# VectorE instead of GpSimd splits the first layer's gate, up and first down weights; two weight copies move ahead of a normalisation

## The chip, the cores and the metric

The kernel runs on one core of a Trainium2 chip. The metric is the device time of one execution in microseconds. A core has a matrix engine (TensorE), three engines for elementwise work (VectorE, ScalarE, GpSimd) and a queue engine (SyncE); each works through its own list of instructions in order, and they wait for each other on semaphores. A weight matrix passes from memory through three of them before TensorE can use it.

## The reference

A trunk of two layers on 512 tokens of width 1024. Each layer has a mixer and a feed-forward part, both with a modulation computed from a vector `c`:

```python
mod = silu(c) @ ada_w[layer] + ada_b[layer]        # six vectors of 1024
x = layer_norm(ALPHA * x + (1 + g_m) * mixer(x * (1 + sc_m) + sh_m))
hf = x * (1 + sc_f) + sh_f
yf = (silu(hf @ w1) * (hf @ w3)) @ w2              # w1, w3: 1024 x 2816, w2: 2816 x 1024
x = layer_norm(ALPHA * x + (1 + g_f) * yf)
```

The change touches the feed-forward part: the gate and up products (`w1`, `w3`) and the down product (`w2`).

## The kernel before

Every operand of TensorE is split into two parts, a high part of lower precision and the low rest; a product is three matmuls (low times high, high times high, high times low). Weights come in slots of 128 x 1024 through rings of four buffers each:

1. SyncE loads a slot into `raw` when the split of the slot four before it is done (`w_lo_ready`).
2. ScalarE copies it to `w_hi` when it has landed and TensorE is done with the slot four before it (`slot_done`); this is the copy (L903).
3. GpSimd computes `w_lo = raw - w_hi`; this is the split (L832).
4. TensorE waits for both.

**The gate and up steps** (`ffn`). Eleven steps per layer, four slots each: slots 0 and 1 hold gate weights, 2 and 3 up weights, for 256 hidden columns. TensorE makes 96 matmuls a step. ScalarE applies silu to the gate (L1261), VectorE multiplies with the up result (L2677, the step's products) and forms four sums of the blocks of the result (L2682 to L2687), which a Strassen-like scheme of seven products for the down matrix needs. For the same scheme VectorE combines four blocks of down weights per step (L2660 to L2666, `combos`); ScalarE issues the load and the store of these.

In the first layer VectorE also computes the second layer's modulation in this loop: four modulation products per step from step 1 on (L2717, L2720), each over a 512 KB slab in one of two buffers `ada_raw`. SyncE's queue in the loop is fixed (L764 to L771): for u = 0 to 3, wait for the split of slot u one step before, load slot u, wait on `ada_step`, load a slab. The slab with number 4j+36+u is loaded when the product of slab 4j+34+u is done, so the weight load of slot 3 of step j comes behind that step's first modulation product, the next step's slots 0, 1 and 2 behind the second, third and fourth.

**The down stage** (`down`). 42 slots per layer (N_DOWN), numbered m from the stage's first slot, of 12 matmuls, or 6 at the short ones. In the first layer GpSimd splits m = 0 to 3 (below LO_FROM) and 30 to 41 (from LO_TO), VectorE the rest; slots 38 and 39 (HELD) go to a place of their own. ScalarE's list there has the copies (`hi`), the high parts of the operands (`b2_hi`, two operations per hidden chunk), and between slots 33 and 36 two normalisations of finished row blocks (`normalize(0)`, `normalize(1)`), each of which waits for VectorE's statistics (L2539).

Of the kernel before, what the change touches and what calls it, by code (L numbers as in the profile page):

```python
# [17 lines left out]
ALU = mybir.AluOpType  # L18
ACT = mybir.ActivationFunctionType
F32 = mybir.dt.float32  # L20
# [19 lines left out]
RING = 4  # L40
# [58 lines left out]
HALF_K = FC // 2  # L99
# [9 lines left out]

DOWN = down_slots()  # L110
N_DOWN = len(DOWN)
LO_FROM, LO_TO = 4, 30
HELD = 38


# [37 lines left out]
SLOTS, N_USED = slot_table()  # L153
# [77 lines left out]
def build_program(nc, wstream, astream, xT, vecs, const, const0, wa_up, dsel, rel, ln_rows, out):  # L231
# [3 lines left out]
    def sem(name):  # L235
        if name not in sems:
            sems[name] = ctx.enter_context(nc.semaphore(name))
        return sems[name]
# [588 lines left out]
    @block.gpsimd  # L827
    def _(pool):
        def split(s, slot):

            pool.wait_ge(sem("w_hi_ready"), s + 1)
            nc.gpsimd.tensor_tensor(w_lo[:, slot, :], raw[:, slot % RAW, :], w_hi[:, slot, :].bitcast(F32),  # L832
                                    ALU.subtract).then_inc(sem("w_lo_ready"), 1)

        assert RAW == RING

        def split_range(a, b):
            if b - a < 2 * RING:
                for s in range(a, b):
                    split(s, s % RING)  # L840
                return
            up, down = -(-a // RING) * RING, b // RING * RING
            for s in range(a, up):
                split(s, s % RING)
            with pool.Fori(up // RING, down // RING) as i:
                for u in range(RING):
                    split(RING * i + u, u)
            for s in range(down, b):
                split(s, s % RING)

        pool.wait_ge(sem("w_lo_ready"), len(FIRST))
        at_ = len(FIRST)
        for x in sorted(list(extra) + [DOWN0, DOWN1]):
            split_range(at_, x)
            at_ = x + 1
            if x in extra:
                pool.wait_ge(sem("w_hi_ready"), x + 1)
                nc.gpsimd.tensor_tensor(extra[x][1], raw[:, x % RAW, :], extra[x][0].bitcast(F32), ALU.subtract
                                        ).then_inc(sem("w_lo_ready"), 1)
                continue  # L860
            for s in range(x, x + LO_FROM):
                split(s, s % RING)
            pool.wait_ge(sem("w_lo_ready"), x + LO_TO)
            for m in range(LO_TO, N_DOWN):
                pool.wait_ge(sem("w_hi_ready"), x + m + 1)
                down_lo(nc.gpsimd, x, m).then_inc(sem("w_lo_ready"), 1)
            at_ = x + N_DOWN
        pool.wait_ge(sem("in_rows"), 16)
        for tb in range(1, TB - 1):
            pool.wait_ge(sem("xh_ready"), TB * 3 + tb + 1)  # L870
            nc.gpsimd.tensor_tensor(x_rows(tb), x_rows(tb), by_chunk(rows_gb[:, 0, :]), ALU.mult).then_inc(sem("scaled"), 1)
            pool.wait_ge(sem("scaled"), tb)
            nc.gpsimd.tensor_tensor(x_rows(tb), x_rows(tb), by_chunk(rows_gb[:, 1, :]), ALU.add).then_inc(sem("out_ready"), 1)
# [3 lines left out]
    def _(act):  # L877
# [41 lines left out]
        def warm_sqrt():  # L919

            nc.scalar.activation(warm[:], eps_col, ACT.Sqrt)
# [261 lines left out]
        def down(layer):  # L1183

            d = SLOTS[f"down{layer}"][0]
            normalize = normalizer(2 * layer + 1)

            def hi(m):
                to_hi(d + m, (d + m) % RING)

            def a_hi(k):

                act.wait_ge(sem("s_step"), 4 * (HALF_K * layer + k + 1))
                if k < 2:
                    act.wait_ge(sem("combo_stored"), 16 * HALF_K * (layer + 1))
                else:
                    act.wait_ge(sem("slot_done"), d + 3 * (k // 2 - 1))
                nc.scalar.activation(a_hl[k % 4][:, 0, :], hid_cols(k, 0, 3), ACT.Copy).then_inc(sem("x_hi_ready"), 1)

            def b1_hi(k):  # L1200

                act.wait_ge(sem("x_ready"), N_SPLIT * layer + SPLIT["a", k])
                nc.scalar.activation(hid_parts(k, 0, 2), hid_cols(k, 3, 2), ACT.Copy).then_inc(sem("x_hi_ready"), 1)

            def b2_hi(k):

                if k == 0:
                    act.wait_ge(sem("slot_done"), d + 15)
                nc.scalar.activation(hid_parts(k, 2), hid_cols(k, 5), ACT.Copy)
                nc.scalar.activation(a22_hi(k), hid_cols(k, 6), ACT.Copy  # L1210
                                     ).then_inc(sem("x_hi_ready"), 1)

            a_hi(0)
            a_hi(1)
            for g in range(6):
                hi(3 * g + 3)
                for k in (2 * g + 2, 2 * g + 3):
                    if k < HALF_K:
                        a_hi(k)
                for k in (2 * g, 2 * g + 1):  # L1220
                    if k < HALF_K:
                        b1_hi(k)
                if g == 5:
                    act.wait_ge(sem("slot_done"), d + 16)
                    for r in range(2):
                        i = nc.scalar.activation(p1_kept(r), by_half(ps[:, 2 * r, :]), ACT.Copy)
                    i.then_inc(sem("p1_copied"), 1)
                hi(3 * g + 4)
                hi(3 * g + 5)
            for k in range(HALF_K):  # L1230
                hi(21 + k)
                b2_hi(k)
            hi(32)
            hi(33)
            warm_sqrt()
            normalize(0)
            hi(34)
            hi(35)
            normalize(1)
            for m in range(36, N_DOWN):  # L1240
                hi(m)
            done[0] = d + N_DOWN
            if layer == 1:
                normalize(2)
                normalize(3)
# [871 lines left out]
    def _(dve):  # L2117
# [528 lines left out]
        def ffn(layer, rest):  # L2646
# [18 lines left out]
                dve.wait_ge(sem("combo_step"), before + 3)  # L2665
                V.tensor_tensor(b21, b21, b11, ALU.subtract).then_inc(sem("combo_step"), 1)  # L2666

            def step(j, between=None):

                combine_weights(j)  # L2670
                if between:
                    between()
                for b in range(2):
                    dve.wait_ge(*((sem("bank_full"), 2 * j + f0) if b == 0 else (sem("slot_done"), 4 * j + (s0 + 4))))
                    dve.wait_ge(sem("silu_ready"), 2 * j + (FC * layer + 1 + b))
                    split = lambda ap: ap.rearrange("q (o a x) -> q o a x", o=1, x=256)
                    V.tensor_tensor(block(j, (slice(0, 5, 4), slice(3, 7, 3))[b]), split(tmp[:, b, :]), split(ps[:, up + b, :]), ALU.mult  # L2677
                                    ).then_inc(sem("prod_ready"), 1)
                a11, s1, s2, a12, a21, s3, a22 = (block(j, a) for a in range(7))
                before = 4 * j + 4 * HALF_K * layer  # L2680
                dve.wait_ge(sem("prod_ready"), 2 * j + (FC * layer + 2))
                V.tensor_tensor(s1, a21, a22, ALU.add).then_inc(sem("s_step"), 1)  # L2682
                V.tensor_tensor(s3, a11, a21, ALU.subtract).then_inc(sem("s_step"), 1)
                dve.wait_ge(sem("s_step"), before + 2)
                V.tensor_tensor(s2, s1, a11, ALU.subtract).then_inc(sem("s_step"), 1)  # L2685
                dve.wait_ge(sem("s_step"), before + 3)
                V.tensor_tensor(a21, a12, s2, ALU.subtract).then_inc(sem("s_step"), 1)  # L2687
# [21 lines left out]

            def two_steps(it, between=None):  # L2710

                for u in range(2):
                    for k in range(4 * u, 4 * u + 4):
                        dve.wait_ge(sem(f"ada_landed{k % 2}"), 64 * it + 16 * (12 + k // 2 + 1))
                        if k:
                            dve.wait_ge(sem("ada_step"), 8 * it + (40 + k))
# [2 lines left out]
                        else:  # L2719
                            V.tensor_scalar(ada_acc[:], ada_raw[:, 0, :], c_act[:, 0:1], None, ALU.mult  # L2720
                                            ).then_inc(sem("ada_step"), 1)
                    if u:
                        dve.wait_ge(sem("ada_step"), 8 * it + 48)
                        fold_rows()
                    step(2 * it + (u + 1), between if u else None)

            with dve.Fori(0, FC // 4 - 1) as it:
                two_steps(it)
# [12 lines left out]
        def down(layer):  # L2741
# [3 lines left out]
            def lo(m):  # L2745

                dve.wait_ge(sem("w_hi_ready"), d + m + 1)
                if m == LO_FROM:
                    dve.wait_ge(sem("w_lo_ready"), d + m)
                down_lo(V, d, m).then_inc(sem("w_lo_ready"), 1)  # L2750

# [11 lines left out]
                                ALU.subtract).then_inc(sem("x_ready"), 1)  # L2763

            for g in range(6):
                if 3 * g + 3 >= LO_FROM:
                    lo(3 * g + 3)
                for k in (2 * g + 2, 2 * g + 3):
                    if k < HALF_K:
# [14 lines left out]
                        ins = V.tensor_tensor(u2_kept(r), p1_kept(r), by_half(ps[:, 5 + 2 * r, :]), ALU.add)  # L2784
                    ins.then_inc(sem("kept_added"), 1)
                lo(3 * g + 5)
            for k in range(HALF_K):
                if 21 + k < LO_TO:
                    lo(21 + k)
                b2_lo(k)  # L2790

        ffn(0, norm(0, "out0"))
        gate_col(1)
# [225 lines left out]
```

## Time and profile before

| | before |
|---|---|
| median of 3 runs | 1326.59 us (1326.4 to 1327.08) |
| profiled execution | 1326.98 us, span 1325.2 us |
| TensorE matmul busy | 1254.8 us (95%) |
| VectorE busy | 901.2 us (68%) |
| ScalarE busy | 528.5 us (40%) |
| GpSimd busy | 476.5 us (36%), 157 splits of 2.54 us on average at L832 |
| chain that ended last | TensorE 60%, issue 17%, GpSimd 9%, VectorE 8%, DMA 3% |

The profiled execution is 0.39 us above the median. Busy shares are averages over stages of different make-up, and a busy matrix engine is not one at its peak, since matmuls overlap. An idle engine costs time only where another one waits for it, so the profile is read stage by stage. The gate and up steps of the first layer lie at about 300 to 545 us of the span, its down stage at 556 to 670, that of the second layer at about 1201 to 1318.

### The profile page before, as it was taken

The page shows a single profiled execution, that of the slowest core. Times are in us where ns is not written, and L with a number is a line of the kernel's source. Part 1 is how long each engine was busy: PE and PEld are TensorE (multiplying, and loading weights), DVE is VectorE, ACT ScalarE, POOL GpSimd, SP SyncE. Part 2 cuts the span into 40 slices and gives each one's busy share as a digit, 9 for nine tenths or more (in the row PEclk, how much of TensorE's full clock was granted, in tenths as well). Part 3 has the DMA queues.
Part 4 walks back from the last instruction along what each step waited for, and adds up shares of the span by engine and source line. Part 5 has one row for each costly group of instructions (what it writes and reads, how often), then busy time and mean ns, then how long its engine had stood idle before and what let it go on. Part 6 is the DMA issues. An engine that isn't in the chain of part 4 may idle for free.

```text
span 1325.2 us, 17193 instructions
## 1 busy us (share of the span) xinstructions
PE 1254.8 (95%) x6298; PEld 1038.9 (78%) x6298; DVE 901.2 (68%) x1244; ACT 528.5 (40%) x767; POOL 476.5 (36%) x195
## 2 busy tenths in 40 slices
PE   7999999998999999599899999999999999999996
PEld 6878887787787778488687777888888888888874
DVE  5489768868778777667766633358697636447785
ACT  3443364542212122366552455527342222225653
POOL 0243332423444444300645332222245444442046
PEclk9999999999999999799999999999999999999998
DMA  9981654534687777557446542212156665645843
GB/s 333 188 175 65 222 160 128 190 112 165 248 286 275 264 281 270 189 152 236 129 164 230 159 124 92 64 63 75 39 176 251 226 233 203 214 173 162 245 151 116
DMA packets 129362, 239.51 MB, mean 181 GB/s; under 512 B 18523, under 2 KB 83307, under 8 KB 126356
## 3 DMA queue, kind: packets, MB, share of 16 engines
q1 hardware_dynamic: 110792, 188.07, 45.5%
q10 hardware_dynamic: 18508, 50.62, 10.5%
q8 instruction: 38, 0.62, 0.2%
q14 instruction: 24, 0.20, 0.0%
HBM read 212.11 MB, written 27.59 MB: 181 GB/s over the span
## 4 chain that ended last, share of the span: by engine, by line
PE 60%; issue 17%; POOL 9%; DVE 8%; DMA 3%; ACT 1%; POOLq 0%; SPq 0%; DVEq 0%; ACTq 0%
PE ps L1391 10%; PE ps L1393 10%; PE ps L1392 10%; POOL w_lo L832 8%; PE ps L1441 4%; PE ps L1442 4%; PE ps L1443 4%; DMA ada_raw<-astream 2%; PE ps L1590 2%; PE ps L1591 2%; PE ps L1592 2%; PE ps L1556 1%; PE ps L1558 1%; PE ps L1557 1%; PE ps L1943 1%
## 5 line engine op out<-in xcount | busy, mean ns | idle before, releaser
L832 POOL TENSOR_TENSOR w_lo<-raw,w_hi 128x1024 fp32r<-128x1024 f32 x157 | 397.7, 2542 | 655.1 <-ACT w_hi L903 654.9
L903 ACT ACTIVATE w_hi<-raw 128x1024 fp32r<-128x1024 f32 (+1 forms) x235 | 238.9, 1031 | 498.2 <-DMA raw<-wstream 181.6
L1391 PE MATMUL ps<-h_lo,w_hi 128*128 128x512 f32 (+2 forms) x1064 | 399.5, 375 | 15.9 <-POOL w_lo L832 13.9
L1393 PE MATMUL ps<-h_hi,w_lo 128*128 128x512 f32 (+2 forms) x1064 | 394.6, 371 | 0.0
L1392 PE MATMUL ps<-h_hi,w_hi 128*128 128x512 f32 (+2 forms) x1064 | 394.6, 371 | 0.0
L1391 PEld LDWEIGHTS ps<-h_lo,w_hi 128*128 128x128 f32 (+1 forms) x1064 | 200.9, 189 | 57.3 <-issue 20.0
L1393 PEld LDWEIGHTS ps<-h_hi,w_lo 128*128 128x128 f32 (+1 forms) x1064 | 200.7, 189 | 34.8
L1392 PEld LDWEIGHTS ps<-h_hi,w_hi 128*128 128x128 f32 (+1 forms) x1064 | 200.9, 189 | 33.2
L650 POOL TENSOR_TENSOR w_lo<-raw,w_hi 128x1024 fp32r<-128x1024 f32 (+1 forms) x20 | 44.6, 2250 | 160.0 <-ACT w_hi L903 159.8
L2717 DVE SCALAR_TENSOR_TENSOR ada_acc<-ada_raw,c_act,ada_acc 128x1024 f32<-128x1024 f32 x35 | 58.8, 1679 | 45.1 <-DMA ada_raw<-astream 44.6
L2677 DVE TENSOR_TENSOR hid<-tmp,ps 128x512 f32<-128x512 f32 (+1 forms) x44 | 29.1, 683 | 86.2 <-PE ps L1393 86.2
L650 DVE TENSOR_TENSOR w_lo<-raw,w_hi 128x1024 fp32r<-128x1024 f32 (+1 forms) x52 | 57.6, 1121 | 30.8 <-ACT w_hi L903 30.4
L1441 PE MATMUL ps<-w_hi,hid_r 128*128 128x512 f32 x160 | 63.9, 400 | 8.2 <-issue 7.6
L2148 DVE SCALAR_TENSOR_TENSOR ada_acc<-ada_raw,c_act,ada_acc 128x1024 f32<-128x1024 f32 x35 | 60.8, 1737 | 12.0 <-DMA ada_raw<-astream 10.1
L1441 PE MATMUL ps<-w_hi,a_hl 128*128 128x512 f32 x132 | 52.5, 398 | 14.4 <-DVE mod L2154 14.4
L1442 PE MATMUL ps<-w_hi,hid_r 128*128 128x512 f32 x160 | 63.6, 398 | 0.0
L1443 PE MATMUL ps<-w_lo,hid_r 128*128 128x512 f32 x160 | 63.6, 398 | 0.0
L1442 PE MATMUL ps<-w_hi,a_hl 128*128 128x512 f32 x132 | 52.2, 395 | 0.0
L1443 PE MATMUL ps<-w_lo,a_hl 128*128 128x512 f32 x132 | 52.1, 394 | 0.0
L2685 DVE TENSOR_TENSOR hid<-hid 128x256 f32<-128x256 f32 (+1 forms) x22 | 48.1, 2186 | 1.6
L1441 PEld LDWEIGHTS ps<-w_hi,hid_r 128*128 128x128 f32 x160 | 30.8, 193 | 16.7 <-issue 9.3
L1590 PE MATMUL ps<-w_hi,h_lo 128*128 128x512 f32 (+1 forms) x112 | 41.8, 373 | 0.7 <-DVE kc L2807 0.7
(318 smaller groups left out, 2033.5 us busy)
## 6 DMA issues: line engine op xcount, KB each, us to landing
raw<-wstream SPq DMA_DIRECT2D x161, 512.0 KB, 4.5
ada_raw<-astream SPq DMA_DIRECT2D x80, 512.0 KB, 4.5
combos<-wstream ACTq DMA_DIRECT2D x22, 1024.0 KB, 5.5
combo_scratch<-combos ACTq DMA_DIRECT2D x22, 1024.0 KB, 3.9
raw<-combo_scratch SPq DMA_DIRECT2D x88, 256.0 KB, 3.3
raw<-wstream SPq DMA_DIRECT2D x66, 256.0 KB, 3.8
ada_first<-astream SPq DMA_DIRECT2D x16, 256.0 KB, 6.7
ada_first<-astream SPq DMA_DIRECT2D x8, 512.0 KB, 10.5
```

The lines of the kernel that those rows point to most:

```text
L650: return engine.tensor_tensor(w_lo[:, s % RING, 0:n], raw[:, s % RAW, 0:n], w_hi[:, s % RING, 0:n].bitcast(F32), ALU.subtract)
L832: nc.gpsimd.tensor_tensor(w_lo[:, slot, :], raw[:, slot % RAW, :], w_hi[:, slot, :].bitcast(F32), ALU.subtract).then_inc(sem("w_lo_ready"), 1)
L903: nc.scalar.activation(w_hi[:, slot, 0:n], raw[:, slot, 0:n], ACT.Copy).then_inc(sem("w_hi_ready"), 1)
L1391: pe.matmul(o, w_h, x_l, start=start, stop=False)
L1392: pe.matmul(o, w_h, x_h, start=False, stop=False)
L1393: return pe.matmul(o, w_l, x_h, start=False, stop=stop)
L1441: pe.matmul(o, x_lo, w_h, start=begin, stop=False, skip_group_check=True)
L1442: pe.matmul(o, x_hi, w_h, start=False, stop=False, skip_group_check=True)
L1443: return pe.matmul(o, x_hi, w_l, start=False, stop=end, skip_group_check=True)
L1590: pe.matmul(o, h_lo[:, k, tokens], w_hi[:, s % RING, w], start=start, stop=False)
L2148: V.scalar_tensor_tensor(ada_acc[:], src, c_act[:, k:k + 1], ada_acc[:], ALU.mult, ALU.add).then_inc(sem("ada_step"), 1)
L2717: V.scalar_tensor_tensor(ada_acc[:], ada_raw[:, k % 2, :], c_act[:, k:k + 1], ada_acc[:], ALU.mult, ALU.add).then_inc(sem("ada_step"), 1)
```

## The change

In the first layer VectorE does the splits of the gate and up slots from the second step on, and of the down slots m = 0 to 3: `step_lo(j, u)` splits slot u of step j, where u = 4 to 6 are the next step's slots 0 to 2. The four modulation products of a step are parted into two pairs (`ada(u, part)`), and the splits stand behind them and behind the combining. GpSimd keeps the first step's four slots. In both layers LO_TO goes from 30 to 32, so that VectorE splits m = 30 and 31 too. ScalarE's copies in the down stage are brought forward: `b2_hi` comes in pairs, slot 34 stands ahead of the first normalisation and slot 36 ahead of the second.

```diff
-LO_FROM, LO_TO = 4, 30
+LO_FROM, LO_TO = 4, 32
@@ GpSimd
-            split_range(at_, x)
+            split_range(at_, x if x != DOWN0 else SLOTS["ffn0"][0] + RING)
...
-            for s in range(x, x + LO_FROM):
-                split(s, s % RING)
+            if x == DOWN1:
+                for s in range(x, x + LO_FROM):
+                    split(s, s % RING)
@@ ScalarE, down
-            for k in range(HALF_K):
-                hi(21 + k)
-                b2_hi(k)
-            hi(32)
-            hi(33)
+            for n in range(6):
+                hi(21 + n)
+                for k in (2 * n, 2 * n + 1):
+                    if k < HALF_K:
+                        b2_hi(k)
+            for m in range(27, 34):
+                hi(m)
             warm_sqrt()
+            hi(34)
             normalize(0)
-            hi(34)
             hi(35)
+            hi(36)
             normalize(1)
-            for m in range(36, N_DOWN):
+            for m in range(37, N_DOWN):
@@ VectorE, ffn
-            def step(j, between=None):
-
+            def step_lo(j, u):
+
+                if layer == 0:
+                    slot = (s0 + u) % RING
+                    dve.wait_ge(sem("w_hi_ready"), 4 * j + (s0 + u + 1))
+                    V.tensor_tensor(w_lo[:, slot, :], raw[:, slot, :], w_hi[:, slot, :].bitcast(F32), ALU.subtract
+                                    ).then_inc(sem("w_lo_ready"), 1)
+
+            def step(j, between=None, beside=None):
+
+                if beside:
+                    beside(0)
+                if not isinstance(j, int) or j:
+                    step_lo(j, 3)
+                elif layer == 0:
+                    dve.wait_ge(sem("w_lo_ready"), s0 + RING)
+                step_lo(j, 4)
                 combine_weights(j)
+                if beside:
+                    beside(1)
+                step_lo(j, 5)
+                step_lo(j, 6)
...
-                for u in range(2):
-                    for k in range(4 * u, 4 * u + 4):
+                def ada(u, part):
+
+                    for k in range(4 * u + 2 * part, 4 * u + 2 * part + 2):
...
+                for u in range(2):
+                    step(2 * it + (u + 1), between if u else None, lambda part: ada(u, part))
@@ VectorE, down
-                if 3 * g + 3 >= LO_FROM:
+                if 3 * g + 3 >= LO_FROM or layer == 0:
                     lo(3 * g + 3)
...
-            for k in range(HALF_K):
-                if 21 + k < LO_TO:
-                    lo(21 + k)
-                b2_lo(k)
+            for n in range(6):
+                lo(21 + n)
+                for k in (2 * n, 2 * n + 1):
+                    if k < HALF_K:
+                        b2_lo(k)
+            for m in range(27, LO_TO):
+                lo(m)
```

VectorE's list in the loop over the first layer's steps, one step up to its products, in the kernel before (`ada_raw`: the slab; `combos`: the down weights that are combined; `hid`: the step's result; register instructions left out):

```order
L2720 TENSOR_SCALAR ada_acc<-ada_raw,c_act 128x1024 [waits ada_landed0]
...
L2717 SCALAR_TENSOR_TENSOR ada_acc<-ada_raw,c_act,ada_acc 128x1024 [waits ada_step]
...
L2660 TENSOR_TENSOR combos<-combos 128x2x256 [waits combo_landed]
...
L2666 TENSOR_TENSOR combos<-combos 128x2x256 [waits combo_step]
...
L2677 TENSOR_TENSOR hid<-tmp,ps 128x2x256
```

The same step after the change:

```order
L2744 TENSOR_SCALAR ada_acc<-ada_raw,c_act 128x1024 [waits ada_landed0]
...
L2741 SCALAR_TENSOR_TENSOR ada_acc<-ada_raw,c_act,ada_acc 128x1024 [waits ada_step]
...
L2677 TENSOR_TENSOR w_lo<-raw,w_hi 128x1024 [waits w_hi_ready]
...
L2677 TENSOR_TENSOR w_lo<-raw,w_hi 128x1024 [waits w_hi_ready]
...
L2664 TENSOR_TENSOR combos<-combos 128x2x256 [waits combo_landed]
...
L2670 TENSOR_TENSOR combos<-combos 128x2x256 [waits combo_step]
...
L2741 SCALAR_TENSOR_TENSOR ada_acc<-ada_raw,c_act,ada_acc 128x1024 [waits ada_step]
...
L2677 TENSOR_TENSOR w_lo<-raw,w_hi 128x1024 [waits w_hi_ready]
...
L2677 TENSOR_TENSOR w_lo<-raw,w_hi 128x1024 [waits w_hi_ready]
...
L2700 TENSOR_TENSOR hid<-tmp,ps 128x2x256
```

All four modulation products stood together at the head of the step and no instruction of the step waited for `w_hi_ready`; now two pairs of splits stand in the list, one behind the first pair of modulation products and one behind the second, and all four wait for ScalarE's copies.

ScalarE's list in the first layer's down stage, from the copy of slot 33 to that of slot 37, before (L921: the table load and a first use of the square root; L1133 to L1149: a normalisation; the last of them is on `xa`):

```order
L903 ACTIVATE w_hi<-raw 128x1024 [waits slot_done,raw_landed2]
L921 ACT_TABLE_LOAD
...
L1133 ACTIVATE cols<-mv,vec_eps 128x1 [waits mv_ready]
...
L1149 ACTIVATE xa<-xa,nmr,rstd 128x8x128 [waits nmr_ready]
L903 ACTIVATE w_hi<-raw 128x1024 [waits slot_done,raw_landed3]
L903 ACTIVATE w_hi<-raw 128x512 [waits slot_done,raw_landed0]
L1133 ACTIVATE cols<-mv,vec_eps 128x1 [waits mv_ready]
...
L903 ACTIVATE w_hi<-raw 128x1024 [waits slot_done,raw_landed1]
```

and after:

```order
L904 ACTIVATE w_hi<-raw 128x1024 [waits slot_done,raw_landed2]
L922 ACT_TABLE_LOAD
...
L904 ACTIVATE w_hi<-raw 128x1024 [waits slot_done,raw_landed3]
L1134 ACTIVATE cols<-mv,vec_eps 128x1 [waits mv_ready]
...
L1150 ACTIVATE xa<-xa,nmr,rstd 128x8x128 [waits nmr_ready]
L904 ACTIVATE w_hi<-raw 128x512 [waits slot_done,raw_landed0]
L904 ACTIVATE w_hi<-raw 128x1024 [waits slot_done,raw_landed1]
L1134 ACTIVATE cols<-mv,vec_eps 128x1 [waits mv_ready]
```

The copy of slot 34 (`raw_landed3`) stands ahead of the first normalisation instead of behind it, that of slot 36 (`raw_landed1`) ahead of the second.

## Rows read from the trace of the kernel before

**Rows 1.** Busy time by stretch: length, then each engine's busy us, clock, DMA share, GB/s.
```profile
318.93:526.12 207.19, 196.03 (x873) 158.56 (x872) 160.16 (x135) 45.92 (x54) 91.95 (x36) 0.98 0.76 271
```
**Rows 2.** Timeline of VectorE: start, length, line, operation, count, idle before and its releaser.
```profile
318.93 0.75 DVE L2720 TENSOR_SCALAR ada_acc<-ada_raw,c_act 128x1024 f32<-128x1024 f32 x1
...
404.40 1.28 DVE L2677 TENSOR_TENSOR hid<-tmp,ps 128x512 f32 x2
...
409.29 2.51 DVE L2687 TENSOR_TENSOR hid<-hid  x1
...
411.79 0.74 DVE L2720 TENSOR_SCALAR ada_acc<-ada_raw,c_act 128x1024 f32<-128x1024 f32 x1
412.56 1.29 DVE L2717 SCALAR_TENSOR_TENSOR ada_acc<-ada_raw,c_act,ada_acc 128x1024 f32<-128x1024 f32 x1
415.94 1.28 DVE L2717 SCALAR_TENSOR_TENSOR ada_acc<-ada_raw,c_act,ada_acc 128x1024 f32<-128x1024 f32 x1 [2.08 <-DMA ada_raw<-astream]
...
427.07 0.69 DVE L2666 TENSOR_TENSOR combos<-combos 128x512 f32<-128x512 f32 x1
...
526.12 2.66 DVE L2717 SCALAR_TENSOR_TENSOR ada_acc<-ada_raw,c_act,ada_acc 128x1024 f32<-128x1024 f32 x2
```
**Rows 3.** Waits of TensorE and VectorE at 320 to 545 us: total, times, longest.
```profile
PE ps L1391 <- POOL w_lo L832: 11.2, 8, 5.7
...
DVE ada_acc L2717 <- DMA ada_raw<-astream: 44.6, 20, 3.3
```
**Rows 4.** Timeline of TensorE, first matmul of a step's fourth slot.
```profile
444.96 0.47 PE L1391 MATMUL ps<-h_lo,w_hi 128*128 128x512 f32 x1 [1.10 <-POOL w_lo L832]
```
**Rows 5.** Source line of a sum: minimum, median and maximum duration in ns.
```profile
L2685 DVE TENSOR_TENSOR hid<-hid x22: 424/2501/2508, 308.9 to 1206.6; 128x256 f32<-128x256 f32 x14, - x8
```
**Rows 6.** Timeline of SyncE's queue in the same step.
```profile
412.56 0.33 SPq L770 DMA_DIRECT2D ada_raw<-astream  x1
413.08 0.33 SPq L767 DMA_DIRECT2D raw<-wstream  x1
...
414.75 0.33 SPq L767 DMA_DIRECT2D raw<-wstream  x1
417.39 0.33 SPq L770 DMA_DIRECT2D ada_raw<-astream  x1
```
**Rows 7.** Source line of VectorE's splits in the down stages, ns.
```profile
L650 DVE TENSOR_TENSOR w_lo<-raw,w_hi x52: 684/1221/1227, 562.7 to 1268.8; 128x1024 fp32r<-128x1024 f32 x42, 128x512 fp32r<-128x512 f32 x10
```
**Rows 8.** Timeline of ScalarE in that step: the copies of two slots.
```profile
418.18 1.06 ACT L903 ACTIVATE w_hi<-raw 128x1024 fp32r<-128x1024 f32 x1 [10.98 <-DMA raw<-wstream]
421.20 1.06 ACT L903 ACTIVATE w_hi<-raw 128x1024 fp32r<-128x1024 f32 x1 [1.96 <-DMA raw<-wstream]
```
**Rows 9.** Timeline of TensorE: the down stage's first matmul.
```profile
556.38 0.77 PE L1441 MATMUL ps<-w_hi,a_hl 128*128 128x512 f32 x1 [14.22 <-DVE mod L2154]
```
**Rows 10.** Timeline of ScalarE and GpSimd in the first layer's down stage.
```profile
633.76 1.06 ACT L903 ACTIVATE w_hi<-raw 128x1024 fp32r<-128x1024 f32 x1 [0.30 <-PE ps L1443]
...
645.77 1.56 ACT L903 ACTIVATE w_hi<-raw 128x1024 fp32r<-128x1024 f32 x2
...
646.89 3.59 POOL L650 TENSOR_TENSOR w_lo<-raw,w_hi 128x1024 fp32r<-128x1024 f32 x2 [8.37 <-ACT w_hi L903]
```
**Rows 11.** Timeline of TensorE there.
```profile
649.33 0.47 PE L1441 MATMUL ps<-w_hi,hid_r 128*128 128x512 f32 x1 [4.79 <-issue]
...
650.42 0.63 PE L1441 MATMUL ps<-w_hi,hid_r 128*128 128x512 f32 x1
650.85 0.63 PE L1442 MATMUL ps<-w_hi,hid_r 128*128 128x512 f32 x1
...
652.98 0.46 PE L1441 MATMUL ps<-w_hi,hid_r 128*128 128x512 f32 x1
```
**Rows 12.** Waits of TensorE in the second layer's down stage, from 1220 us.
```profile
PE ps L1441 <- issue: 2.8, 2, 2.1
```
**Rows 13.** Source line of the loop's 40 weight loads: us to landing.
```profile
DMA to landing us min/median/max: 3.4/5.1/6.8
```
**Rows 14.** DMA issues by line: times, KB each, median us to landing.
```profile
combo_scratch<-combos ACTq DMA_DIRECT2D x22, 1024.0 KB, 3.9
```

More of the change, by code:

```diff
@@ L2721, in two_steps @@
                                             ).then_inc(sem("ada_step"), 1)
-                    if u:
+                    if u and part:
                         dve.wait_ge(sem("ada_step"), 8 * it + 48)
                         fold_rows()
-                    step(2 * it + (u + 1), between if u else None)
+                for u in range(2):
+                    step(2 * it + (u + 1), between if u else None, lambda part: ada(u, part))
             with dve.Fori(0, FC // 4 - 1) as it:
@@ L2747, in lo @@
                 dve.wait_ge(sem("w_hi_ready"), d + m + 1)
-                if m == LO_FROM:
+                if m == LO_FROM and layer == 1:
                     dve.wait_ge(sem("w_lo_ready"), d + m)
```

## The prediction

> **What bounds the kernel now.** I read first the busy time by stretch, because an average over the whole span says nothing about one loop. Over nine gate/up steps of the first layer, from the second step's first modulation product (318.93) to the last step's (526.12), TensorE is busy 196.0 of 207.2 us [rows 1]. A step is therefore (526.12 - 318.93) / 9 = 23.02 us long [rows 2]. Next I read who waits. TensorE waits for a GpSimd split, 11.2 us in 8 waits [rows 3]; the one at 444.96 is 1.10 us [rows 4]. So TensorE's own need is about 23.1 - 1.1 = 22.0 us, and the difference is the most this loop can give back to it.
>
> Then I read VectorE in order of time, since all that changes in the loop is on it. VectorE hardly ever waits for TensorE here; it waits for its own modulation loads, 44.6 us in 20 waits [rows 3]. It goes round a circle of its own. The products of a step at 404.40 are followed by two sums of about 2.5 us each, though such a sum takes 0.42 us at its shortest, and the next step's first modulation product, whose start I call T, follows at 411.79 [rows 2, 5].
>
> Last I read SyncE's queue. It issues in one fixed order: a weight load, a modulation load, a weight load, and so on. A modulation load waits until VectorE has consumed the one two before it, and the weight load behind it in the queue waits too. The rows show it: the first product ends at 411.79 + 0.74 = 412.53; at 412.56 a modulation load goes out and at 413.08 the weight load of the step's fourth slot. The second product ends at 413.85, and the next weight load goes out at 414.75; the third product starts only at 415.9, and the pair behind it at 417.39 [rows 2, 6]. Weights are loaded at the pace of VectorE's modulation products. So far nothing on VectorE waits for those weights, because GpSimd takes the splits.
>
> **The change, part by part: the loop.** It adds four splits per step to VectorE, 1.22 us each at the median [rows 7]. It takes GpSimd away from beside VectorE, so I let the two sums fall from 2.5 to 0.42 us, and VectorE's way from the products to the next T from 411.79 - 404.40 = 7.4 to 7.4 - 2 x 2.05 = 3.3 us [rows 2, 5]. By busy time alone VectorE would then fit well inside 22 us. The price is in the waits: each split waits for ScalarE's copy, which waits for a load, and on VectorE all else stands behind the split: the combining of the down weights, the remaining modulation products, the products of the step and so the next T.
>
> In the new order a step is: modulation products 1 and 2, split of its slot 3, split of the next step's slot 0, combining, modulation products 3 and 4, splits of the next slots 1 and 2, the step's own products, the sums. From T, with the times of the step at 411.79:
> - modulation product 2 ends at 0.77 + 1.29 = 2.06 [rows 2]. The weight load behind it goes out at 414.75 - 411.79 = 2.96 [rows 6]. It has landed when ScalarE starts its copy, at 421.20 - 411.79 = 9.41, which is 6.45 us after issue; the copy takes 1.06, to 10.47 [rows 8]. The split ends at about 11.7. (The load of slot 3 is a trip of 418.18 - 413.08 = 5.10 us; its split, done at 8.7, lies inside this one.)
> - combining: four operations of 0.69 us [rows 2], with their gaps 2.9, to 14.6.
> - modulation products 3 and 4, 1.29 each, to 17.2. Only now can the loads of the other two slots go out; the last one 0.9 us behind, at 18.1.
> - that load is again the fourth of four, so I give it the same 6.45 us: 24.55. Copy 25.6, split 26.9.
> - then 3.3 us to the next T: 30.2 us. A step whose first product is of the longer kind comes out a little under that, since less follows its sums. I take 30.1.
>
> Two load trips that stood beside VectorE's work would now stand in it, one after the other. TensorE needs 22.0 of the 30, so its own waits, two of about 4 us per step, cost nothing more.
>
> Nine steps: 9 x (30.1 - 23.02) = +63.7 us. Step 0 has no modulation products and its loads are early: two sums shorter by 2.05 each against three splits of 1.22 and some waiting for copies; I take -1, between -4 and +3. After the last T: before, the first down product starts at 556.38, 30.3 us behind it, with 14.22 us of TensorE waiting for VectorE's last block [rows 9]. After, by the same steps: splits of two slots to 13, combining 15.9, two modulation products 18.5, the fold 19.7, two splits 22.2, the low parts of the first operands 24.2, products, sums and block 27.5 (fold and low parts are estimates, 1.2 and 1.0 each, by the split's rate). That is -2.8. The down weights are queued behind no modulation load, so no second trip is paid there.
>
> **The down stages, both layers.** Before, ScalarE made the copy of slot 34 only behind the first row block's normalisation, at 645.77, though it had finished slot 33's at 633.76 + 1.06 = 634.8; GpSimd's split followed at 646.89, and TensorE stood 4.79 us until 649.33 [rows 10, 11]. From there its matmuls started 0.43 us apart, half the full clock, and ten rows took 3.65 us where nine gaps of 0.23 take 2.05: 1.6 more [rows 11]. Moved ahead of the normalisation the copy can start when slot 30 is done, one slot (12 matmuls, 2.7 us) after slot 33's copy was let go, at 636.5; GpSimd has two splits less before it, and with three of 2.5 us from 633.5 is done near 641, before TensorE asks at 644.5. What is late next is slot 37, whose copy stays behind the second normalisation; VectorE should reach both normalisations earlier, its low parts no longer held up by GpSimd, so I expect no wait from it. That is -6.4. In the second layer the same waits are 2.8 us [rows 12]: -2.8. At the least they are worth nothing, if slot 37 or a later one takes the wait over. I take -9.2, bounds 0 and -9.2.
>
> Sum against the profiled execution's own 1326.98 us, 0.39 above the median of the runs: 63.7 - 1 - 2.8 - 9.2 = +50.7, so 1377.7. I predict 1377.
>
> **What is unknown is the length of the two trips.** No row shows the second burst as it will be. The forty weight loads of this loop landed after 3.4 us at least, 5.1 at the median and 6.8 at most [rows 13]. With 5.1 for both trips a step is 30.1 - 2 x 1.35 = 27.4, 24 us less in all: 1353. With the store of the combined weights (3.9 us [rows 14], issued at T + 14.7) ahead of the second burst for the 2.6 us that it still needs then, 23 us more: 1401. I take 6.45 because it is the row of a load in the same place, last of four.
>
> The Trainium skill ("DMA: Bandwidth & Descriptors", section "Anatomy of one DMA — SWDGE (gpsimd) path") gives a transfer about 2 us fixed and its bytes at 436 GB/s. For 512 KB that is an estimate of 3.2 us; by it the step would be 23.6 us and the kernel 8 us faster. It was fitted on GpSimd's queue; the row of the last of four is twice that, and the sum goes by the row.
>
> **Rivals.**
> - *Short trips.* If the loads land as the shortest did, a step is 30.1 - 2 x 3.05 = 24.0: +8.8 - 13.0, so 1323, faster. It decides at 23.02 + 13.0 / 9 = 24.46 us a step, a trip of 3.6 us. For it: a longer step packs its loads less tightly. Against: minimum 3.4, median 5.1, and four loads would still go out within 2.2 us. Chance 0.08.
> - *The waits are covered.* If weight loads ran ahead of the modulation products, TensorE would set the step at 22.0: -9.2 - 13.0, so 1305. Against: SyncE's order is untouched. Chance 0.03.
> - *Median trips*, 1353: 0.15. *Store in the way*, 1401: 0.15.
> - *The clock.* Twice a step TensorE would idle about 4 us, and after 4.79 it ran at 1.2 GHz [rows 11]. If it stayed there, 96 matmuls at 0.43 are 41 us a step: 9 x 18.3 - 13.0, so 1478. Against: in that row's place the full clock was back within 4 us, and two such spells (+3.2 us) hide in a step of 30. Chance 0.03. The skill's "TensorE: Matmul & The Clock Gate" (section "Part 1: The HAM clock gate (the “warmup” mystery)") has the idle engine at 1.2 GHz and gives 2.4 back after sustained work; the trace agrees on both.
>
> **How the numbers follow.** The forecast, with its own range 1362 to 1390, has 0.56. Slower by over 0.2% (2.7 us, about what runs of this kernel can tell from no change): the forecast, median trips, store and clock, together 0.89. Faster 0.09, the first two rivals but for the part of short trips near the turning point, 0.02, that would be within. The range 1342 to 1402 takes in the two bounds of the trips and leaves out the fast cases and the clock, 0.14.
>
> **What would show it.** In the changed profile: T to T near 30 us; VectorE idle before its splits, some 7 us in each of two places per step, put down to ScalarE's copies, and those waiting for weight loads; TensorE idle about 4 us twice a step; sums at 0.42; no 4.8 us wait in the down stage. The prediction is wrong if T to T is under 24.5, or if the copies are ready before VectorE comes to the splits.

## The result, and the profile after

The changed kernel takes 1380.32 us (1378.59 to 1380.59, 4 runs) against 1326.84 in the same comparison: ratio 1.040, 95% interval 1.038 to 1.042. It is slower by 53.5 us; 1377 was predicted. The profiled execution has a span of 1378.5 us.

The first view is again the busy time by stretch, over the same nine steps of the loop (length, then each engine's busy time, clock, DMA share, GB/s), the answer to [rows 1]:

```profile
318.33:593.88 275.55, 219.10 (x887) 173.82 (x887) 141.03 (x170) 46.84 (x54) 0.00 (x0) 0.92 0.58 206
```

A step is 275.55 / 9 = 30.62 us, against 23.02. GpSimd is silent. VectorE does four more splits per step and still has less busy time than before (141.03 against 160.16), since what was stretched beside GpSimd is short again, the sums first of all: the median of the one in [rows 5] falls from 2501 ns to 426. TensorE waits, and its clock is at full speed less often: about the same number of matmuls takes 219 us in place of 196. The second view is the waits of the same stretch (total, times, longest), the answer to [rows 3]:

```profile
ACT w_hi L904 <- DMA raw<-wstream: 234.0, 36, 15.0
DVE w_lo L2677 <- ACT w_hi L904: 128.2, 36, 6.8
...
PE ps L1395 <- DVE w_lo L2677: 38.4, 14, 4.8
...
PE ps L1608 <- DVE ada_part L2162: 16.2, 4, 4.5
```

Read upward it is one chain: TensorE waits for VectorE's splits, these for ScalarE's copies, these for weight loads. VectorE's wait for modulation loads, 44.6 us before, is gone: they have landed long before it asks.

The third view is one step of VectorE in order of time, the answer to [rows 2]:

```profile
379.70 0.76 DVE L2744 TENSOR_SCALAR ada_acc<-ada_raw,c_act 128x1024 f32<-128x1024 f32 x1
380.49 1.28 DVE L2741 SCALAR_TENSOR_TENSOR ada_acc<-ada_raw,c_act,ada_acc 128x1024 f32<-128x1024 f32 x1
386.65 1.23 DVE L2677 TENSOR_TENSOR w_lo<-raw,w_hi 128x1024 fp32r<-128x1024 f32 x1 [4.88 <-ACT w_hi L904]
389.80 1.23 DVE L2677 TENSOR_TENSOR w_lo<-raw,w_hi 128x1024 fp32r<-128x1024 f32 x1 [1.92 <-ACT w_hi L904]
...
393.12 0.69 DVE L2670 TENSOR_TENSOR combos<-combos 128x512 f32<-128x512 f32 x1
393.73 2.60 DVE L2741 SCALAR_TENSOR_TENSOR ada_acc<-ada_raw,c_act,ada_acc 128x1024 f32<-128x1024 f32 x2
402.77 1.23 DVE L2677 TENSOR_TENSOR w_lo<-raw,w_hi 128x1024 fp32r<-128x1024 f32 x1 [6.45 <-ACT w_hi L904]
405.93 1.23 DVE L2677 TENSOR_TENSOR w_lo<-raw,w_hi 128x1024 fp32r<-128x1024 f32 x1 [1.93 <-ACT w_hi L904]
407.07 1.28 DVE L2700 TENSOR_TENSOR hid<-tmp,ps 128x512 f32 x2
...
410.33 1.28 DVE L2741 SCALAR_TENSOR_TENSOR ada_acc<-ada_raw,c_act,ada_acc 128x1024 f32<-128x1024 f32 x1
```

The reader is to see two places where VectorE stands, 6.80 and 8.38 us, each behind a pair of modulation products. SyncE's queue (answer to [rows 6]) and ScalarE's copies (to [rows 8]) say what it stands for:

```profile
380.48 0.33 SPq L770 DMA_DIRECT2D ada_raw<-astream  x1
381.01 0.33 SPq L767 DMA_DIRECT2D raw<-wstream  x1
381.80 0.33 SPq L770 DMA_DIRECT2D ada_raw<-astream  x1
382.67 0.33 SPq L767 DMA_DIRECT2D raw<-wstream  x1
395.18 0.33 SPq L770 DMA_DIRECT2D ada_raw<-astream  x1
395.70 1.04 SPq L767 DMA_DIRECT2D raw<-wstream  x1
396.84 1.14 SPq L770 DMA_DIRECT2D ada_raw<-astream  x1
398.17 0.33 SPq L767 DMA_DIRECT2D raw<-wstream  x1
```

```profile
388.71 1.06 ACT L904 ACTIVATE w_hi<-raw 128x1024 fp32r<-128x1024 f32 x1 [2.09 <-DMA raw<-wstream]
...
404.84 1.06 ACT L904 ACTIVATE w_hi<-raw 128x1024 fp32r<-128x1024 f32 x1 [2.10 <-DMA raw<-wstream]
```

Each burst of four loads starts when the first product of a pair is done (380.46 and about 395.0), and the copy of the last one starts 6.04 us (382.67 to 388.71) and 6.67 us (398.17 to 404.84) after its issue.

The other stretches are read from where stages begin on TensorE. The first row answers [rows 9], the second is late in that layer's down stage (the first matmul behind a block of those on xa), the third begins the second layer's:

```profile
620.71 0.76 PE L1445 MATMUL ps<-w_hi,a_hl 128*128 128x512 f32 x1 [6.86 <-DVE mod L2158]
...
725.47 0.48 PE L1445 MATMUL ps<-hid_r 128*128 128x512 f32 x1
...
1260.26 0.47 PE L1445 MATMUL ps<-w_hi,a_hl 128*128 128x512 f32 x1 [0.22 <-DVE mod L2158]
```

The same two places in the kernel before:

```profile
667.87 0.48 PE L1441 MATMUL ps<-hid_r 128*128 128x512 f32 x1
...
1202.53 0.47 PE L1441 MATMUL ps<-w_hi,a_hl 128*128 128x512 f32 x1 [0.22 <-DVE mod L2154]
```

Between these places, the 53.3 us between the spans (1378.5 - 1325.2) split up as follows (T, as before, is a step's first modulation product):

| stretch | before | after | difference | predicted |
|---|---|---|---|---|
| start to the first T | 318.93 | 318.33 | -0.6 | -1 |
| nine steps | 207.19 | 275.55 | +68.4 | +63.7 |
| last T to first down product | 30.26 | 26.83 | -3.4 | -2.8 |
| down stage, layer 0, to that late matmul | 111.49 | 104.76 | -6.7 | -6.4 |
| from there to down stage, layer 1 | 534.66 | 534.79 | +0.1 | 0 |
| down stage, layer 1, and end | 122.67 | 118.24 | -4.4 | -2.8 |

### The profile page after: what moved, and what is told of

It reads as the page before. It is cut to its first block, busy times and chain, and to the rows that moved or that the text cites. A ratio compares the mean times of both kernels' runs of the same rounds, so it can differ in the third digit from the quotient of the medians.

```text
span 1378.5 us, 17156 instructions
## 1 busy us (share of the span) xinstructions
PE 1271.5 (92%) x6298; PEld 1050.4 (76%) x6298; DVE 873.2 (63%) x1292; ACT 529.3 (38%) x767; POOL 353.4 (26%) x147
## 4 chain that ended last, share of the span: by engine, by line
PE 58%; DVE 15%; DMA 10%; issue 8%; POOL 3%; ACT 3%; SPq 2%; DVEq 0%; POOLq 0%; ACTq 0%
PE ps L1395 9%; PE ps L1396 9%; PE ps L1397 9%; DMA raw<-wstream 9%; PE ps L1445 4%; PE ps L1446 4%; PE ps L1447 4%; DVE ada_acc L2741 2%; ACT w_hi L904 2%; POOL w_lo L832 2%; PE ps L1594 2%; PE ps L1596 2%; PE ps L1595 2%; SPq L770 1%; DVE hid L2700 1%
## 5 line engine op out<-in xcount | busy, mean ns | idle before, releaser
L1395 PE MATMUL ps<-h_lo,w_hi 128*128 128x512 f32 (+2 forms) x1064 | 407.5, 383 | 45.3 <-DVE w_lo L2677 39.6
L832 POOL TENSOR_TENSOR w_lo<-raw,w_hi 128x1024 fp32r<-128x1024 f32 x113 | 284.4, 2525 | 491.2 <-ACT w_hi L904 491.2
L1396 PE MATMUL ps<-h_hi,w_hi 128*128 128x512 f32 (+2 forms) x1064 | 401.6, 377 | 0.0
L1397 PE MATMUL ps<-h_hi,w_lo 128*128 128x512 f32 (+2 forms) x1064 | 401.3, 377 | 0.0
L1395 PEld LDWEIGHTS ps<-h_lo,w_hi 128*128 128x128 f32 (+1 forms) x1064 | 205.5, 193 | 90.4 <-issue 53.0
L650 POOL TENSOR_TENSOR w_lo<-raw,w_hi 128x1024 fp32r<-128x1024 f32 (+1 forms) x16 | 33.8, 2136 | 499.8 <-ACT w_hi L904 499.8
L2677 DVE TENSOR_TENSOR w_lo<-raw,w_hi 128x1024 fp32r<-128x1024 f32 x43 | 52.5, 1223 | 137.6 <-ACT w_hi L904 137.6
L650 DVE TENSOR_TENSOR w_lo<-raw,w_hi 128x1024 fp32r<-128x1024 f32 (+1 forms) x57 | 63.6, 1127 | 34.9 <-ACT w_hi L904 34.2
L2152 DVE SCALAR_TENSOR_TENSOR ada_acc<-ada_raw,c_act,ada_acc 128x1024 f32<-128x1024 f32 x35 | 63.2, 1807 | 12.3 <-DMA ada_raw<-astream 10.4
L2741 DVE SCALAR_TENSOR_TENSOR ada_acc<-ada_raw,c_act,ada_acc 128x1024 f32<-128x1024 f32 x35 | 44.9, 1282 | 1.3 <-DVE ada_acc L2744 0.5
L1596 PE MATMUL ps<-w_lo,h_hi 128*128 128x512 f32 (+1 forms) x112 | 40.4, 360 | 0.0
```

What stands on the lines that cost most here:

```text
L650: return engine.tensor_tensor(w_lo[:, s % RING, 0:n], raw[:, s % RAW, 0:n], w_hi[:, s % RING, 0:n].bitcast(F32), ALU.subtract)
L1395: pe.matmul(o, w_h, x_l, start=start, stop=False)
L1396: pe.matmul(o, w_h, x_h, start=False, stop=False)
L1397: return pe.matmul(o, w_l, x_h, start=False, stop=stop)
L1596: m = pe.matmul(o, h_hi[:, k, tokens], w_lo[:, s % RING, w], start=False, stop=stop)
L2741: V.scalar_tensor_tensor(ada_acc[:], ada_raw[:, k % 2, :], c_act[:, k:k + 1], ada_acc[:], ALU.mult, ALU.add).then_inc(sem("ada_step"), 1)
```

## The experiments

The theory: VectorE's own line now holds two load trips per step, because the weight loads stand behind modulation loads in SyncE's queue, and these wait for VectorE's modulation products. The rivals: VectorE's added work itself makes the step longer; the load traffic is too slow whatever its order; the store of the combined weights is in the way of the second burst.

**The two parts apart.** down_only takes the loop's part back (below, against the changed kernel); loop_only does the opposite, with the down stages of before.

```diff
-            split_range(at_, x if x != DOWN0 else SLOTS["ffn0"][0] + RING)
+            split_range(at_, x)
...
-            def step_lo(j, u):
...
-                step_lo(j, 5)
-                step_lo(j, 6)
```

> The part for the down stages alone (slots 30 and 31 to VectorE, copies ahead of the normalisation, low parts in pairs); in the gate/up loop GpSimd splits as before, and the first four down slots too. Two trips in VectorE's line (my theory): the whole loss is the loop's, so this kernel keeps the steps of 23.0 us and gains what the down stages gain, 9 us by the forecast's terms (6.4 and 2.8): 1317.5, ratio to before 0.993. Rival, the down part only moves its wait to slot 37 or later and after's loss is a smaller loop loss alone: ratio 1.000.

> The loop's part alone: VectorE splits the gate/up weights and the first four down slots; the order of the down stages as before. My theory: nine steps of 30.6 us against 23.0 (+68.4), 3.4 less behind the last, 1 less in the first: 1391, ratio 1.048. Rival, the two parts need each other (the down stage gets slower or faster only with VectorE's splits of its first four slots): down_only and loop_only do not add up to the whole change's +53.5; they miss it by more than 4 us.

Measured: down_only 1315.54 us, ratio 0.991 (0.989 to 0.992); loop_only 1391.82, ratio 1.048 (1.046 to 1.050). The differences, -12.0 and +64.3, add up to +52.3, 1.2 us from the +53.5 of both and inside the 4 us that the expectation allowed. The whole loss is the loop's, and the down part is a gain of its own, 3 us more than was expected of it (see the next section).

**The tie cut.** lead_two leaves every instruction of VectorE where the change put it and only lets the weight loads run two places ahead of the modulation loads:

```diff
+        LEAD = 2
+        for u in range(LEAD):
+            load(s0 + 4 + u)
...
-        with sp.Fori(1, FC // 2) as j:
+        with sp.Fori(1, FC // 2 - 1) as j:
             for u in range(4):
-                sp.wait_ge(sem("w_lo_ready"), 4 * j + (s0 + u - RAW + 1))
-                sp.dma_start(raw[:, (s0 + u) % RAW, :], wstream[bass.ds(4 * j + (s0 + u + store_of("ffn0")), 1)].rearrange("s p n -> p (s n)")
-                             ).then_inc(sem(f"raw_landed{(s0 + u) % RAW}"), 16)
+                ahead(j, u + LEAD)
...
+        for u in range(4):
+            if u < 4 - LEAD:
+                load(s0 + 4 * (FC // 2 - 1) + u + LEAD)
+            load_ada(4 * (FC // 2 - 1) + 36 + u)
```

Here ahead(j, u) holds the wait and the load taken out, for slot u of step j. lead_one is the same with LEAD = 1.

> The changed kernel with SyncE's queue reordered in the loop: every weight load stands two modulation loads earlier (slots 2 and 3 of a step and 0 and 1 of the next in one round), so it goes out about half a step before its split is needed. VectorE's instructions and their order are those of the changed kernel. Theory of the two trips: the loads have about 11 us for trips of 6 to 6.7, VectorE waits for no copy, TensorE sets the step at about 22.0 us: nine steps give 77.6 us back, 1303, ratio to before 0.982. Rival, VectorE's added work itself (four splits of 1.22 us and their semaphores) is what lengthens the step: it stays at 30.6 and the kernel at 1380, ratio 1.040. Rival, the load traffic itself is too slow whatever its order: between the two, 1340 to 1370.

> As lead_two, but each weight load only one modulation load earlier. Theory of the two trips: the last load of each of the two bursts goes out one modulation product and its issue earlier, 1.5 us in the first and 1.4 to 2.5 in the second, so both trips still stand in VectorE's line and the step is 27 to 28 us: 1347 to 1357, ratio 1.015 to 1.023. Rivals: VectorE's work 1380, as for lead_two; if one place of lead is already enough to cover a trip, 1303 to 1325.

Measured: lead_two 1291.25 us, ratio 0.973 (0.971 to 0.974), 89 us under the changed kernel. Busy time over the loop's first two steps and the four behind them (from T to T), and the top of the waits from 318 to 507 us:

```profile
318.00:353.49 35.49, 35.49 (x164) 29.13 (x164) 31.00 (x38) 8.56 (x10) 0.00 (x0) 1.00 0.89 322
...
353.49:441.22 87.73, 87.73 (x402) 72.12 (x401) 62.95 (x77) 21.78 (x24) 0.00 (x0) 1.00 0.82 300
```

```profile
ACT w_hi L915 <- PE ps L1408: 86.9, 21, 4.8
ACT tmp L1276 <- PE ps L1408: 28.4, 15, 2.1
DVE w_lo L2688 <- ACT w_hi L915: 21.7, 12, 3.3
```

TensorE is busy for the whole of 87.73 us, 21.93 us a step, which is the need of 22.0 worked out before (the 23.1 in that sum is the time from this row of the kernel before to the one in [rows 4], 444.96 - 421.84):

```profile
421.84 0.47 PE L1391 MATMUL ps<-h_lo,w_hi 128*128 128x512 f32 x1 [0.88 <-POOL w_lo L832]
```

VectorE does the same splits and is busy 15.7 us of a step; the longest waits are now those for TensorE. The rival of VectorE's work falls. So does slow traffic: the loads move 300 GB/s here against 206, and a median one takes as long as in the changed kernel (5.9 us there),

```profile
DMA to landing us min/median/max: 3.3/6.0/8.1
```

but TensorE doesn't wait for it, and ScalarE only three times, 13.5 us in all. lead_two beat the forecast of 1303 by 12. Of this, 8.5 us are in the first row: VectorE enters the loop behind TensorE, and the first two steps from T to T take 35.49 us and not 44, while it catches up (TensorE makes 164 matmuls in these two, 402 in the four behind them, and has no idle time in either). The forecast had counted all nine at TensorE's rate.

lead_one: 1325.68 us, ratio 0.998 (0.997 to 0.999), against 1347 to 1357 expected, so the direction held and the size didn't. The time lies 0.7 us beyond the range of the rival that one place covers a trip, so it is the rows that decide between the two. A step is (540.11 - 318.02) / 9 = 24.68 us. Four rows of one step, SyncE's first and ScalarE's second, with T at 415.99:

```profile
417.30 0.36 SPq L770 DMA_DIRECT2D raw<-wstream  x1
...
428.57 1.05 SPq L770 DMA_DIRECT2D raw<-wstream  x1
```

```profile
421.58 1.06 ACT L915 ACTIVATE w_hi<-raw 128x1024 fp32r<-128x1024 f32 x1 [6.50 <-DMA raw<-wstream]
...
434.39 1.06 ACT L915 ACTIVATE w_hi<-raw 128x1024 fp32r<-128x1024 f32 x1 [5.88 <-DMA raw<-wstream]
```

The expectation counted only that a load goes out one place earlier. But the load waited for is now also the second of its burst and no longer the fourth, and its trip is shorter: 4.28 and 5.82 us instead of 6.04 and 6.67. Two trips still stand in VectorE's line, at 6.50 and 5.88 us of ScalarE waiting, so the rival falls. That a trip's length depends on the place in the burst called for the next two runs.

**What makes a trip long.** small_mod cuts the bytes that lie ahead of the last load; small_store cuts the store beside the second burst to an eighth.

```diff
-                sp.dma_start(ada_raw[:, u % 2, :], astream[bass.ds(4 * j + (36 + u), 1)].rearrange("s p n -> p (s n)")
+                sp.dma_start(ada_raw[:, u % 2, 0:128], astream[bass.ds(4 * j + (36 + u), 1)].rearrange("s p n -> p (s n)")[:, 0:128]
```

> The changed kernel with each modulation load of the loop cut to 128 of 1024 columns (the output leaves out the rest of these rows); their number, order and semaphores stay. It asks why the last load of a burst takes 6 to 6.7 us where the second of a burst took 4.3 in lead_one. If it waits for the bytes ahead of it (3 x 512 KB), the trip falls to about 4.3: both together 4.1 us less per step, 26.5 us, nine steps -37: 1343, ratio to before 1.012. If the trip is a fixed latency of a load, nothing changes: 1380, ratio 1.040.

```diff
-            act.dma_start(combo_dram[at_] if isinstance(j, int) else combo_dram[bass.ds(at_, 1)].rearrange("s p n -> p (s n)"),
-                          combos[:].rearrange("q a x -> q (a x)")).then_inc(sem("combo_stored"), 16)
+            n = 2048 if isinstance(j, int) or layer else 256
+            act.dma_start((combo_dram[at_] if isinstance(j, int) else combo_dram[bass.ds(at_, 1)].rearrange("s p n -> p (s n)"))[:, 0:n],
+                          combos[:].rearrange("q a x -> q (a x)")[:, 0:n]).then_inc(sem("combo_stored"), 16)
...
-        if combined:
+        if combined and layer:
```

> The changed kernel with the store of the first layer's combined down weights cut to 256 of 2048 columns (and the first layer's down stage loads uncombined panels of the same size, so that its output leaves out the combination there). It asks how much of the second burst's length (6.67 us for its last load against 6.04 in the first, and two issues of over 1 us on SyncE instead of 0.33) is the 1 MB store issued 1.2 us before it. If the store makes both differences, a step loses 0.6 + 1.4 = 2.1 us: nine steps 19 us, 1361, ratio to before 1.026. If the trip is the burst's own, no change: 1380, ratio 1.040.

Measured: small_mod 1341.23 us, ratio 1.011 (1.009 to 1.012), a step of (555.89 - 316.69) / 9 = 26.58 us: 1343 and 26.5 were expected. One last load of a first burst, issue and copy:

```profile
426.77 0.33 SPq L767 DMA_DIRECT2D raw<-wstream  x1
```

```profile
430.88 1.06 ACT L904 ACTIVATE w_hi<-raw 128x1024 fp32r<-128x1024 f32 x1 [1.31 <-DMA raw<-wstream]
```

4.11 us, against 6.04 with full loads ahead of it. The long trips go with the other loads' bytes and are no fixed latency; what is left with the two small loads is the other weight load and whatever is fixed.

small_store: 1370.57 us, ratio 1.033 (1.031 to 1.034), a step of 29.55: 1.07 us less, half of what the store was charged with. (In the ninth step, outside the loop, the store keeps its size.) The second burst of one step, and the copy that ends it:

```profile
452.29 0.33 SPq L767 DMA_DIRECT2D raw<-wstream  x1
452.94 0.33 SPq L770 DMA_DIRECT2D ada_raw<-astream  x1
453.46 0.33 SPq L767 DMA_DIRECT2D raw<-wstream  x1
```

```profile
460.04 1.06 ACT L904 ACTIVATE w_hi<-raw 128x1024 fp32r<-128x1024 f32 x1 [2.53 <-DMA raw<-wstream]
```

The two long issues are gone, and they were the store's: the last load goes out 1.4 us earlier in the step (17.1 us behind T at 436.40, against 18.5). But its trip is 6.58 us, as with the store (6.67). So the store makes the last load go out later, and the load's own trip no longer. Whether SyncE's issue time alone does this isn't shown: from its first issue to the copy of its last load the burst takes 9.66 us with the store (395.18 to 404.84) and 8.28 without (451.76 to 460.04), and the first burst, with no store beside it, takes 8.23, though its last load goes out 0.5 us later behind its first than here. The store's bytes may take their share of the traffic, and no run parts the two.

**The queue without VectorE's splits.** lead_gpsimd is down_only with the queue of lead_two.

> down_only with the queue order of lead_two: GpSimd splits in the loop, the weight loads go out half a step earlier. It asks whether the gain of lead_two is the queue's alone or needs VectorE's splits. If the queue's order alone sets it, TensorE's waits for GpSimd splits (11 us before) go and the time is 1306 or, with all that lead_two gained, 1291: ratio 0.973 to 0.985. If GpSimd's splits of 2.5 us beside VectorE, and the sums that take 2.5 us beside them, hold the step at 23.0 us, it stays with down_only at 1315, ratio 0.991.

Measured: 1308.28 us, ratio 0.986 (0.984 to 0.988), between its two answers. The queue alone is worth 7 us over down_only; VectorE's splits on top of it another 17. TensorE's waits from 255 to 545 us in this kernel name one of the places:

```profile
PE ps L1405 <- POOL w_lo L843: 6.2, 1, 6.2
```

It waits 6.2 us once for a GpSimd split, and later, ahead of the down stage, 13.20 us for VectorE's last block; lead_two has none of the first and 6.40 of the second (first row lead_gpsimd, second lead_two):

```profile
548.44 0.76 PE L1455 MATMUL ps<-w_hi,a_hl 128*128 128x512 f32 x1 [13.20 <-DVE mod L2168]
...
532.45 0.77 PE L1456 MATMUL ps<-w_hi,a_hl 128*128 128x512 f32 x1 [6.40 <-DVE mod L2169]
```

Together that is 13.0 of the 17 us; the other 4 were not followed up.

lead_two beats both kernels: 36 us under the one before, 2.7%.

## Why the prediction was right

The sign, the place and the mechanism held, and the step can be laid beside its forecast, in us behind T (379.70 above): second modulation product done 2.07 (forecast 2.06); last load of the first burst issued 2.97 (2.96), its split done 11.33 (11.7); combining done 14.1 (14.6); products 3 and 4 done 16.6 (17.2); last load of the second burst issued 18.47 (18.1), its split done 27.46 (26.9); next T 30.63 (30.2). The sums are at 0.42 us as forecast.

- **The trips.** 6.45 us was taken for both from a load in the same place of the queue [rows 8]; they came out at 6.04 and 6.67 in this step, together 0.2 us off, and at 5.95 and 6.41 on average over the nine. Part of the closeness is luck: the one row read was the longest of its kind (the last of four took 5.5 to 6.4 us in the other steps of the kernel before), and what it gave too much covers part of the issue time that the sum left out (next point). The median trip of 5.1 [rows 13] would have been wrong because it mixes loads from all places of a burst; lead_one and small_mod show that the bytes ahead of a load set most of its trip. The fixed cost and byte rate in the Trainium skill ("DMA: Bandwidth & Descriptors", section "Anatomy of one DMA — SWDGE (gpsimd) path") make an estimate of 3.2 us for 512 KB. The shortest landing of small_mod's weight loads, 3.1 us, is close to it; the last of four full loads took twice as long, and there the measurement decides:

```profile
DMA to landing us min/median/max: 3.1/4.1/4.9
```

- **The loop came out at +68.4, not +63.7: the term that was sized too small.** In the step above the forecast is short by 0.9 us in one item, the issue of the second burst: its last load goes out 1.8 us behind the products, where 0.9 was taken from the first burst. The store issued just ahead of it makes two of SyncE's issues take 1.04 and 1.14 us; small_store shows that with an eighth of it they take 0.33. The store was among the rivals, priced as 2.6 us of longer landing; the seven eighths taken away in small_store are worth 1.07 us a step, by a later last load and no longer trip.
- **TensorE's waits.** Two of some 4 us per step were forecast. There are 14 of 38.4 us in all, and four more, 16.2 us, in the product that folds the modulation (L1608), which were not foreseen: every second step it stands in TensorE's order ahead of the gate/up matmuls, and VectorE comes to its fold late. They cost nothing of their own, since VectorE sets the step; with lead_two they are gone.
- **The clock**, a rival at 0.03, came in part: over the loop the granted clock falls from 0.98 to 0.92, and matmuls behind a wait take 0.63 and 0.77 us in place of 0.39. TensorE's busy time is 23 us longer (14 more matmuls are in it too), but in a step that VectorE sets.
- **The down stages.** Layer 0 gave 6.7 where 6.4 was worked out. ScalarE's rows there, the answer to [rows 10], have the copy of slot 34 ahead of the normalisation that it stood behind:

```profile
701.62 1.06 ACT L904 ACTIVATE w_hi<-raw 128x1024 fp32r<-128x1024 f32 x1
703.08 0.29 ACT L1134 ACTIVATE cols<-mv,vec_eps 128x1 f32<-128x1 f32 x1 [0.40 <-DVE mv L2543]
...
710.38 1.04 ACT L904 ACTIVATE w_hi<-raw 128x1024 fp32r<-128x1024 f32 x1
```

  The last of these is slot 37's, where the wait could have gone; TensorE has none there. The first normalisation now waits 0.40 us for VectorE's statistics, against 7.33 in the kernel before:

```profile
643.68 0.30 ACT L1133 ACTIVATE cols<-mv,vec_eps 128x1 f32<-128x1 f32 x1 [7.33 <-DVE mv L2539]
```

  The prediction had expected that. It also means that the wait had two remedies in one edit, the copy's new place and VectorE's earlier statistics, and no run parts them. Layer 1 gave 4.4 and not 2.8, because only the wait was counted there. The rows before show a slow stretch behind it, as in layer 0:

```profile
1290.58 0.47 PE L1441 MATMUL ps<-w_hi,hid_r 128*128 128x512 f32 x1 [2.12 <-issue]
...
1292.13 0.63 PE L1443 MATMUL ps<-w_lo,hid_r 128*128 128x512 f32 x1
1292.56 0.63 PE L1441 MATMUL ps<-w_hi,hid_r 128*128 128x512 f32 x1
...
1294.69 0.46 PE L1443 MATMUL ps<-w_lo,hid_r 128*128 128x512 f32 x1
```

From 1292.13 to 1292.56 is 0.43 us a matmul, against 0.23 at full clock; the eleven gaps from 1290.58 to 1294.69 take 4.11 us where 2.5 would do, and that is the missing 1.6. The loop's loss and the down part's larger gain erred in opposite ways, which is part of why the total is 3 us off and the loop 5.

## What to carry to other kernels

Before work is moved to another engine, look at what that engine's results release: here VectorE's products released the loads that its new splits needed, and the loop grew by a third though VectorE's busy time fell. Work that is cheap in busy time still costs the whole wait of its slowest input on an in-order engine, so move the load first and the work second: with the loads two places earlier in the queue the same change gains 36 us instead of losing 53. For the length of such a wait take the trip of a load in the same place of its burst, not a median.

## What was not expected of the hardware

- A load's landing time goes with the bytes issued ahead of it: a 512 KB load was copied 6.0 and 6.7 us after issue as the last of four full loads (5.6 to 6.9 over the nine steps), 4.3 as the second (5.8 where the 1 MB store went ahead), and 4.1 as the last of four when two of the others ahead were 64 KB.
- A 1 MB store issued by ScalarE about 1.2 us before makes two load issues on SyncE take 1.04 and 1.14 us instead of 0.33; with the store cut to an eighth they take 0.33, and the last load's trip stays the same (6.58 against 6.67).
